# A bias row multiplied in the indexer's first visit, the last query heads turned one chunk later, one output part stored from ScalarE's queue

## The chip, the core and the metric

The kernel runs on one core of a Trainium2 chip. The core has five engines that run side by side, each through its own list of instructions in order: TensorE (PE, matmuls; its weight loads are shown apart as PEld), VectorE (DVE), ScalarE (ACT), GpSimd (POOL) and SyncE (SP, which here only issues DMAs). They meet in semaphores: an instruction can wait until a semaphore has reached a value, and can raise one when it ends. The metric is the device time of one execution in microseconds (us), lower is better.

## What is computed

Two transformer-like blocks in float32 over 256 rows of 2048 numbers. The first block has three branches (a windowed mean, a short convolution, and attention over the 64 keys that an indexer scores highest), gates, an output projection and an MLP. The second has attention with a Fourier mix beside it, and a last norm. What the change touches:

```
# block 1: the bias of a head depends on the distance of query and key alone
dist = q_pos[None, :, None] - idx
bias = table[t5_bucket(dist)]                      # table is rel_bias, 32 buckets x 8 heads
...
# block 1: the indexer
dots = einsum('bthd,bsd->bths', q_idx, k_idx)
score = einsum('bth,bths->bts', w_idx * IDX_HEADS ** -0.5, relu(dots))
...
# block 2
q = rope(rmsnorm(heads(p, OFF_Q, 12), q_norm_g), cos, sin) * q_scale
y = fft.fftn(u_b, axes=(rows, 128 columns of a group), norm="ortho").real
...
return rmsnorm(xs, final_g)                        # 256 x 2048, the output
```

## The kernel before

**Chunks.** All large products are cut into jobs of 512 weight columns, and a job into chunks of 256 weight rows (KC = 2 tiles of 128). `chunks` is the list of all of them, `q` is a chunk's number; `of[name].first` and `of[name].end` are the numbers of a job's first chunk and of the one behind its last. The weights of a chunk are loaded by SP into one of five buffers `raw`, in the order of the list `loads`, in which the 96 loads of `w_ada_2` (ada loads) stand between the others. ScalarE rounds them to float32r (`high`, tile `whiW` or `whiT`), VectorE subtracts that from them (`low`, tile `wloW` or `wloT`), and TensorE multiplies high by high, high by low and low by high: three matmuls for one product (lines 876 to 878, or 869 to 871 where the rows are the stationary side). One chunk of the first kind is 24 matmuls of 256 columns.

**The ring.** There are four pairs of high and low buffers. ScalarE's `high(q)` waits until the chunk four before it is multiplied (`s_pe`) and until its load has landed. SP's load of an entry waits until the entry five before it in `loads` has been read by VectorE (`s_lo` for weights, `s_ada` for an ada load). The loops of ScalarE and VectorE run three chunks ahead (AHEAD = 3): in step q each does first the side work that its table lists for q, then `high(q + 3)` or `low(q + 3)`, then what an ada load calls for (`ada`, four operations of 512 columns), then the end of a job. TensorE does the side work of q just ahead of chunk q.

**Side work.** Three tables written out by hand, `pe_at`, `act_at` and `dve_at`, say in which step a small piece stands. The pieces that the change touches or that stand beside them:

- `bias_row`: one float32 matmul of the 32 x 8 table with a 32 x 384 one-hot matrix (`oneh`, loaded by GpSimd at the start) gives the bias of every distance in bank 4. VectorE copies it to `erow` (line 1345) and raises `s_erow_v`, GpSimd stores it to HBM (line 556) and raises `s_erow_w`, and later GpSimd spreads it into a table (line 560) and loads that (line 564).
- `index_dots(u)`, `index_relu(u)`, `index_sum(u)`: the indexer in twelve units, two to a visit, from chunk `of["vw"].end + 1` = 33 on, every four chunks. Unit 0 of `index_dots` waits for `s_erow_v`, since it writes the bank that the bias row stood in; unit 0 of `index_sum` waits for `s_erow_w`, since the scores `sc` lie where `erow` lay.
- `turn_qk(s, tt)`: four 128 x 128 transposes that turn the heads of a query job; `s == 4` is the job `qq2`, the last four heads. They are first used by `scores2(8)`, in step `of["ga0"].first + 3`.
- `fourier_t(g)` and `fourier_d(g)`: the two products of the Fourier mix of a group.

"Visit" is used here for a stretch in which TensorE leaves the chunks for side work.

**The end.** The last chunks are `o23`. VectorE and ScalarE scale the rows of `X2` by the last norm's factor, `s_fin` counts VectorE's parts and `s_fina` ScalarE's (line 1220), and SP stores five parts (line 514), each as its wait is met, in the order in which they are listed.

Of the kernel before, what the change touches and what calls it, by code (L numbers as in the profile page):

```python
# [132 lines left out]
def program(nc, a, out, scratch_e, scratch_x):  # L133
    ctx = ExitStack()
    with ctx:
# [5 lines left out]
        chunks, of, given = [], {}, [0, 0]  # L141
# [29 lines left out]
        pe_at, act_at, dve_at = defaultdict(list), defaultdict(list), defaultdict(list)  # L171

        def side(table, q, part, *arg):
            table[q].append((part, arg))
# [7 lines left out]
        for u in range(3, 8):  # L182
            side(act_at, u - 2, "turn_x", u)
            side(dve_at, u - 2, "turn_x", u)
        side(pe_at, 7, "bias_row")
        side(dve_at, 8, "bias_row")
        units = [(1, par, i) for par in range(2) for i in range(4)] + [(0, par, i) for par in range(2) for i in range(2)]
        for u in range(12):
            q = of["vw"].end + 1 + 4 * (u // 2)
# [6 lines left out]
        for g in range(4):  # L196
            q = of["vw"].end + 11 + 4 * g
# [7 lines left out]
        for i in range(4):  # L205
            q = of["q1"].end + 2 + 10 * i
# [18 lines left out]
        for tt in range(2):  # L225
            q = of["wo0"].first + 3 + 2 * tt
# [3 lines left out]
            q = of["wo3"].end + 1 + tt  # L230
# [3 lines left out]
            q = of["dn33"].end + 1 + tt  # L234
            side(dve_at, q, "mlp_add", tt)
            q = of["dn33"].end + 2 + tt
# [8 lines left out]
        for s, name in enumerate(("kc", "k", "qq0", "qq1", "qq2")):  # L245
            q = of[name].end
            for tt in range(2):
                side(act_at, q + tt, "scale_qk", s, tt)
                if s:
                    side(dve_at, q + tt, "rotate", s, tt)  # L250
                side(pe_at, q + (7 if s == 3 else 5), "turn_qk", s, tt)
                side(act_at, q + (7 if s == 3 else 5), "turn_qk", s, tt)
        heads2 = [of["za0"].first + 6, of["qq1"].first + 5, of["za1"].end, of["zb"].first + 1, of["ga0"].first + 3, of["ga0"].first + 10]
        for i in range(6):
            q = heads2[i]
# [10 lines left out]
        for g in range(4):  # L266
            q = of["zb"].end + 2 + 3 * g
# [13 lines left out]
        def at(name, shape, off, dt=F32):  # L281
            return nc.alloc_sbuf_tensor_at(name, shape, dt, offset=off)
# [36 lines left out]
        a5 = tmp[5]  # L319
# [8 lines left out]
        def bg(name, shape, kb, dt=F32):  # L328
            return at(name, shape, big + int(kb * 1024), dt)
# [18 lines left out]
        x0 = bg("x0", [128, 2, 2048], 52)  # L348
        yah, yal = bg("yah", [128, 8, 256], 52, F32R), bg("yal", [128, 8, 256], 60, F32R)
        cm = bg("cm", [128, 2, 256], 68)  # L350
        oneh = bg("oneh", [128, 384], 70)
        vst = bg("vst", [128, 128], 71.5)
        quart = bg("quart", [128, 8, 2, 16], 70.5)
        foldm = bg("foldm", [128, 128], 71.5)
# [1 line left out]
        erow = bg("erow", [128, 384], 22)  # L356
# [40 lines left out]
        bank = [ctx.enter_context(nc.psum_tensor(f"ps{i}", [128, 512], F32)) for i in range(8)]  # L397
# [9 lines left out]
        def sem(name):  # L407
            return ctx.enter_context(nc.semaphore("s_" + name))
# [16 lines left out]
        s_turn, s_turned, s_oper = sem("x_turned"), sem("x_scaled"), sem("x_operand")  # L425
        s_skew, s_erow, s_erow_v, s_erow_w, s_bt = sem("bias_copies"), sem("bias_row"), sem("bias_row_read"), sem("bias_row_stored"), sem("bias_table")
# [23 lines left out]
        s_fgb, s_o2v, s_o2sq, s_o2g, s_fin, s_fina = (  # L450
            sem("final_gain"), sem("x3_rows"), sem("x3_square"), sem("x3_gained"), sem("out_rows0"), sem("out_rows1"))
        s_out = [sem(f"out{i}") for i in range(5)]
# [10 lines left out]
        def norm_col(name, tt):  # L463

            w = 4 if name in QK else 1
            c = col(f"n_{name}{tt}", 2 * w)
            return c[:, 0:w], c[:, w:2 * w]
# [5 lines left out]
        @block.sync  # L473
        def _(sp):
            def rows_of(x, tt):
                return a[x][0, 128 * tt:128 * tt + 128, :]

            for t in range(2):
                sp.dma_start(x0[:, t, :], rows_of("x", t)).then_inc(s_x[t], 16)
            sp.dma_start(ident[:, :], a["k_ident"]).then_inc(s_ident, 16)  # L480
            sp.dma_start(vst[0:64, :], a["norm_gains"].rearrange("l g (r c) -> (l g r) c", c=128)).then_inc(s_va, 16)
            sp.dma_start(vst[64:112, :], a["b_gate"].rearrange("l g (r c) -> (l g r) c", c=128)).then_inc(s_va, 16)
            for i, (kind, m) in enumerate(loads):
                if i == 4:
                    r0 = 0
                    for name, n, pat in (("pool_scale", 8, "l (r c) -> (l r) c"), ("conv_w", 24, "l k (r c) -> (l k r) c"),
                                         ("norm_g_2", 16, "l (r c) -> (l r) c"), ("q_norm_g_2", 1, None), ("k_norm_g_2", 1, None),
                                         ("c_2", 16, "l (r c) -> (l r) c"), ("c_ctx_2", 16, "(r c) -> r c")):
                        sp.dma_start(vsu[r0:r0 + n, :], a[name] if pat is None else a[name].rearrange(pat, c=128)).then_inc(s_vb, 16)
                        r0 += n  # L490
                    sp.dma_start(vsu[82:114, :], a["b_ada_2"][:, 0:4096].rearrange("l (r c) -> (l r) c", c=128)).then_inc(s_vb, 16)
                if i >= NRAW:
                    was, mm = loads[i - NRAW]
                    if was == "w":
                        sp.wait_ge(s_lo, mm + 1)
                    else:
                        sp.wait_ge(s_ada, mm + 1)
                if kind == "w":
                    job, k = chunks[m]
                    o = 0  # L500
                    for c0, cn in job.cols:
                        sp.dma_start(raw[i % NRAW][:, 0:KC, o:o + cn], job.w[:, k:k + KC, c0:c0 + cn]).then_inc(s_raw[i % NRAW], 16)
                        o += cn
                else:
                    j, k = m // 8, m % 8 * KC
                    wa = a["w_ada_2"][0].rearrange("(k p) n -> p k n", p=128)
                    sp.dma_start(raw[i % NRAW][:, :, :], wa[:, k:k + KC, 512 * j:512 * j + 512]).then_inc(s_raw[i % NRAW], 16)
            rows = out[0].rearrange("(t p) n -> p t n", p=128)
            for i, (tt, c0, c1) in enumerate(((0, 1536, 2048), (0, 0, 1536), (1, 1536, 2048), (1, 0, 768), (1, 768, 1536))):
                if i == 3:  # L510
                    sp.wait_ge(s_fina, 1)
                else:
                    sp.wait_ge(s_fin, (1, 2, 3, 0, 4)[i])
                sp.dma_start(rows[:, tt, c0:c1], X2[:, tt, c0:c1]).then_inc(s_out[i], 16)
            for i in range(5):
                sp.wait_ge(s_out[i], 16)
# [112 lines left out]
        def _(pe):  # L629
# [43 lines left out]
            def bias_row():  # L673
                pe.wait_ge(s_oneh, 16)
                pe.wait_ge(s_relb, 16)
                pe.wait_ge(s_oper, 8)
                pe.matmul(bank[4][0:8, 0:384], a5[0:32, 0:8], oneh[0:32, :], start=True, stop=True).then_inc(s_erow, 1)

            def ada_fold():

# [235 lines left out]
        def _(act):  # L916
# [287 lines left out]
            def ep_o2(job, b0, b1):  # L1204
                c = job.arg
                for tt in range(2):
                    if c == 3 and tt == 1:
                        for i in range(2):
                            act.wait_ge(s_o2v, 8 + i)
                            act.activation(tmp[3][:, 256 * i:256 * i + 256], X2[:, 1, 1536 + 256 * i:1792 + 256 * i], ACT.Square,  # L1210
                                           accum_out=col("x3_halves")[:, i:i + 1]).then_inc(s_o2sq, 1)
                        break
                    act.wait_ge(s_o2v, 2 * c + tt + 1)
                    act.activation(tmp[2 * (c % 2) + tt][:, :], X2[:, tt, 512 * c:512 * c + 512], ACT.Square,
                                   accum_out=ss_all[:, 2, tt, c:c + 1]).then_inc(s_o2sq, 1)
                if c == 3:
                    act.wait_ge(s_rstd, norm_no["x3", 1])
                    act.wait_ge(s_o2g, 6)
                    x = X2[:, 1, 0:768]
                    act.activation(x, x, ACT.Copy, scale=norm_col("x3", 1)[1]).then_inc(s_fina, 1)  # L1220

            eps = {"copy": ep_copy, "kk": ep_kk, "vw": ep_vw, "pool": ep_pool, "cu": ep_cu, "cb": ep_cb, "gate": ep_gate, "br": ep_br,
                   "wo": ep_wo, "up": ep_up, "dn": ep_dn, "qk": ep_qk, "v": ep_v, "silu": ep_silu, "gate2": ep_gate2, "pa": ep_pa, "o2": ep_o2}
# [6 lines left out]
            for i in range(3):  # L1230
# [4 lines left out]
                if i == 1:  # L1235
                    act.wait_ge(s_rstd, 2)
                    x = x0[:, 1, 512:1024]
# [14 lines left out]
        def _(v):  # L1252
# [89 lines left out]

            def bias_row():
                v.wait_ge(s_erow, 1)
                v.tensor_copy(erow[0:8, :], bank[4][0:8, 0:384]).then_inc(s_erow_v, 1)

            def index_sum(u):
                tt, par, i = units[u]
# [511 lines left out]
```

## Time and profile before

| what | value |
|---|---|
| median of three executions | 2211.5 us (2211.46 to 2211.52) |
| profiled execution, its own time | 2211.45 us |
| its span in the profile | 2209.7 us |
| TensorE busy | 2200.9 us, 100% of the span |
| VectorE busy | 1503.4 us, 68% |
| ScalarE busy | 1066.5 us, 48% |
| GpSimd busy | 63.1 us, 3% |
| share of TensorE in the chain that ended last | 99% |

How to read it: the profile shows one execution. A row of the timeline gives start, duration, engine, line of the kernel, what is written and read, how many instructions were put together, and in square brackets how long the engine sat idle just before and what ended that. Matmuls overlap in their pipeline, so the distance between two starts is what one costs, not its duration. The span is what the profile covers; 1.8 us of the execution lie outside it.

### The profile page before, as it was taken

Reading aid. Unit: us, or ns where it says so; the run is one execution under the profiler, and the core shown is the slowest. Engines: PE = TensorE matmul, PEld = TensorE weight load, DVE = VectorE, ACT = ScalarE, POOL = GpSimd, SP = SyncE. Lnnn points to the kernel's source line nnn. Section 1 sums busy time; section 2 is a strip of 40 time slices with the busy share of each in tenths; the row PEclk is TensorE's granted clock in tenths of the full one; section 3 lists DMA queues with packets and bytes.
Section 4 is the critical chain, followed back from the end, with each engine's and each line's share of the span. In section 5 each row is a group of like instructions: output and inputs, shape, how many; then the busy total and the mean of one; then the engine's idle time right before and its main releaser. Section 6 shows DMA issues by size and latency. Waiting matters only on the chain.

```text
span 2209.7 us, 37880 instructions
## 1 busy us (share of the span) xinstructions
PE 2200.9 (100%) x16074; PEld 2069.7 (94%) x16074; DVE 1503.4 (68%) x1901; ACT 1066.5 (48%) x1417; POOL 63.1 (3%) x72
## 2 busy tenths in 40 slices
PE   9999999999999999999999999999999999999998
PEld 9999999999999889989988988988889999999987
DVE  7789588888889657544554555555756556577776
ACT  5444445544444546444443443444656555544443
POOL 1000000000000000000000000000100000010001
PEclk9999999999999999999999999999999999999999
DMA  8876676787787756656656666666664445678784
GB/s 275 241 224 209 192 248 219 231 281 259 252 277 269 234 181 186 196 191 190 200 191 194 188 200 202 196 195 200 227 204 139 135 144 171 213 265 294 252 279 157
DMA packets 248034, 474.99 MB, mean 215 GB/s; under 512 B 21527, under 2 KB 26001, under 8 KB 247097
## 3 DMA queue, kind: packets, MB, share of 16 engines
q1 hardware_dynamic: 243032, 454.40, 64.4%
q0 software_dynamic: 4832, 18.16, 2.5%
q8 instruction: 126, 2.06, 0.4%
q14 instruction: 44, 0.35, 0.0%
HBM read 468.30 MB, written 5.78 MB: 215 GB/s over the span
## 4 chain that ended last, share of the span: by engine, by line
PE 99%; issue 0%; DVE 0%; ACT 0%; POOLq 0%; POOL 0%; DVEq 0%
PE ps L876 21%; PE ps L878 21%; PE ps L877 21%; PE ps L869 11%; PE ps L870 11%; PE ps L871 11%; PE ps L793 1%; PE ps L697 1%; PE ps L666 0%; PE ps L782 0%; PE ps L890 0%; PE ps L772 0%; PE ps L773 0%; PE ps L709 0%; PE ps L755 0%
## 5 line engine op out<-in xcount | busy, mean ns | idle before, releaser
L876 PE MATMUL ps<-op0h,whiW 128*128 128x256 f32 x3376 | 937.5, 278 | 0.0
L878 PE MATMUL ps<-op0h,wloW 128*128 128x256 f32 x3376 | 932.3, 276 | 0.0
L877 PE MATMUL ps<-op0l,whiW 128*128 128x256 f32 x3376 | 932.2, 276 | 0.0
L1263 DVE TENSOR_TENSOR wloW<-raw,whiW 128x1024 fp32r<-128x1024 f32 (+1 forms) x503 | 611.1, 1226 | 342.3 <-ACT whiW L923 339.9
L923 ACT ACTIVATE whiW<-raw 128x1024 fp32r<-128x1024 f32 (+1 forms) x504 | 529.4, 1058 | 582.1 <-PE ps L878 479.3
L876 PEld LDWEIGHTS ps<-op0h,whiW 128*128 128x128 f32 x3376 | 633.7, 188 | 2.2 <-issue 1.6
L877 PEld LDWEIGHTS ps<-op0l,whiW 128*128 128x128 f32 x3376 | 633.8, 188 | 0.6
L878 PEld LDWEIGHTS ps<-op0h,wloW 128*128 128x128 f32 x3376 | 633.7, 188 | 0.0
L1263 DVE TENSOR_TENSOR wloT<-raw,whiT 128x1024 fp32r<-128x1024 f32 (+1 forms) x264 | 317.4, 1212 | 258.8 <-ACT whiT L923 258.2
L923 ACT ACTIVATE whiT<-raw 128x1024 fp32r<-128x1024 f32 (+1 forms) x264 | 273.8, 1047 | 293.3 <-PE ps L871 244.1
L869 PE MATMUL ps<-whiT,op1h 128*128 128x512 f32 x640 | 249.2, 389 | 0.0
L870 PE MATMUL ps<-wloT,op1h 128*128 128x512 f32 x640 | 249.0, 389 | 0.0
L871 PE MATMUL ps<-whiT,op1l 128*128 128x512 f32 x640 | 249.0, 389 | 0.0
L1291 DVE SCALAR_TENSOR_TENSOR tmp<-raw,csil,tmp 128x512 f32<-128x512 f32 x300 | 209.4, 747 | 2.5 <-DMA raw<-in_w_ada 1.3
L871 PEld LDWEIGHTS ps<-whiT,op1l 128*128 128x128 f32 x640 | 120.1, 188 | 25.0
L869 PEld LDWEIGHTS ps<-whiT,op1h 128*128 128x128 f32 x640 | 120.1, 188 | 24.8
L870 PEld LDWEIGHTS ps<-wloT,op1h 128*128 128x128 f32 x640 | 120.1, 188 | 24.7
L876 PE MATMUL ps<-op1h,whiW 128*128 128x256 f32 x512 | 142.0, 277 | 0.0
L877 PE MATMUL ps<-op1l,whiW 128*128 128x256 f32 x512 | 141.4, 276 | 0.0
L878 PE MATMUL ps<-op1h,wloW 128*128 128x256 f32 x512 | 141.4, 276 | 0.0
L877 PEld LDWEIGHTS ps<-op1l,whiW 128*128 128x128 f32 x512 | 96.1, 188 | 0.1
L876 PEld LDWEIGHTS ps<-op1h,whiW 128*128 128x128 f32 x512 | 96.1, 188 | 0.1
(286 smaller groups left out, 2041.8 us busy)
## 6 DMA issues: line engine op xcount, KB each, us to landing
raw<-in_w_in SPq DMA_DIRECT2D x256, 512.0 KB, 4.4
raw<-in_w_up SPq DMA_DIRECT2D x128, 512.0 KB, 3.8
raw<-in_w_down SPq DMA_DIRECT2D x128, 512.0 KB, 3.8
raw<-in_w_ada SPq DMA_DIRECT2D x96, 512.0 KB, 4.6
raw<-in_w_gate SPq DMA_DIRECT2D x96, 512.0 KB, 5.1
raw<-in_w_out SPq DMA_DIRECT2D x64, 512.0 KB, 5.0
raw<-in_w_branch SPq DMA_DIRECT2D x48, 512.0 KB, 4.9
raw<-in_w_proj_a SPq DMA_DIRECT2D x24, 512.0 KB, 5.0
```

Of the source, the lines that this page charges most:

```text
L697: mm = pe.matmul(ps[:, j * nk:(j + 1) * nk], qb[lo:lo + 64, h // 2, 128 * tt:128 * tt + 128], kid[lo:lo + 64, 0:nk], start=True, stop=True)
L793: mm = pe.matmul(ps[:, 128 * tt:128 * tt + 128], vv[:, st % 2, 128 * kv:128 * kv + 128], p[:, 128 * st:128 * st + 128], start=st == 0, sto ...
L869: pe.matmul(o, th, h[:, kk, c0:c1], start=first, stop=False, skip_group_check=True)
L870: pe.matmul(o, th, l[:, kk, c0:c1], start=False, stop=False, skip_group_check=True)
L871: mm = pe.matmul(o, tl, h[:, kk, c0:c1], start=False, stop=last, skip_group_check=True)
L876: pe.matmul(o, wh, xh[:, ka, :], start=first and m % 2 == 0, stop=False, skip_group_check=True)
L877: pe.matmul(o, wh, xl[:, ka, :], start=False, stop=False, skip_group_check=True)
L878: mm = pe.matmul(o, wl, xh[:, ka, :], start=False, stop=last, skip_group_check=True)
L923: act.activation(whi[job.mode][q % NSPL][:, :, 0:job.n], raw[i][:, :, 0:job.n], ACT.Copy).then_inc(s_hi, 1)
L1263: v.tensor_tensor(wlo[job.mode][q % NSPL][:, :, 0:job.n], x, h.bitcast(F32), ALU.subtract).then_inc(s_lo, 1)
L1291: op = v.scalar_tensor_tensor(o, w, c, o, ALU.mult, ALU.add)
```

## The change

There are four edits. `bias_row` goes from step 7 to step 33 on TensorE (ahead of the first `index_dots`) and from step 8 to step 34 on VectorE, and writes bank 7 in place of bank 4; its wait for the x operand is dropped, and `oneh` gets another place in memory. `turn_qk` of the last heads goes from the fifth to the sixth chunk behind `qq2`, on TensorE and on ScalarE. The part of the output that ScalarE scales is stored by ScalarE itself. SP stores the other four.

```diff
-        side(pe_at, 7, "bias_row")
-        side(dve_at, 8, "bias_row")
+        side(pe_at, of["vw"].end + 1, "bias_row")
+        side(dve_at, of["vw"].end + 2, "bias_row")
...
-                side(pe_at, q + (7 if s == 3 else 5), "turn_qk", s, tt)
-                side(act_at, q + (7 if s == 3 else 5), "turn_qk", s, tt)
+                side(pe_at, q + (7 if s == 3 else 6 if s == 4 else 5), "turn_qk", s, tt)
+                side(act_at, q + (7 if s == 3 else 6 if s == 4 else 5), "turn_qk", s, tt)
...
-        oneh = bg("oneh", [128, 384], 70)
+        oneh = bg("oneh", [128, 384], 30.25)
...
-            for i, (tt, c0, c1) in enumerate(((0, 1536, 2048), (0, 0, 1536), (1, 1536, 2048), (1, 0, 768), (1, 768, 1536))):
-                if i == 3:
-                    sp.wait_ge(s_fina, 1)
-                else:
-                    sp.wait_ge(s_fin, (1, 2, 3, 0, 4)[i])
+            for i, (tt, c0, c1) in enumerate(((0, 1536, 2048), (0, 0, 1536), (1, 1536, 2048), (1, 768, 1536))):
+                sp.wait_ge(s_fin, i + 1)
...
                 pe.wait_ge(s_relb, 16)
-                pe.wait_ge(s_oper, 8)
-                pe.matmul(bank[4][0:8, 0:384], a5[0:32, 0:8], oneh[0:32, :], start=True, stop=True).then_inc(s_erow, 1)
+                pe.matmul(bank[7][0:8, 0:384], a5[0:32, 0:8], oneh[0:32, :], start=True, stop=True).then_inc(s_erow, 1)
...
                     act.activation(x, x, ACT.Copy, scale=norm_col("x3", 1)[1]).then_inc(s_fina, 1)
+                    act.wait_ge(s_fina, 1)
+                    act.dma_start(out[0, 128:256, 0:768], x).then_inc(s_out[4], 16)
...
                 v.wait_ge(s_erow, 1)
-                v.tensor_copy(erow[0:8, :], bank[4][0:8, 0:384]).then_inc(s_erow_v, 1)
+                v.tensor_copy(erow[0:8, :], bank[7][0:8, 0:384]).then_inc(s_erow_v, 1)
```

The line of `index_dots(0)` that waits for `s_erow_v` is not touched, nor that of `index_sum(0)` that waits for `s_erow_w`.

In the listings below a row gives line, operation, written tile, read tiles, size, and in brackets the semaphores it waits for. `s_bias_row` is `s_erow`, `s_bias_row_read` is `s_erow_v`, and `s_bias_row_stored` is `s_erow_w`.

TensorE at the step from chunk 32 to chunk 33, before (`kid,qb` is `index_dots`):

```order
670 L876 MATMUL ps<-op0h,whiW_55 128x256
671 L877 MATMUL ps<-op0l,whiW_55 128x256
672 L878 MATMUL ps<-op0h,wloW_63 128x256
673 L697 MATMUL ps<-kid,qb 128x256 [waits s_pair0_read,s_bias_row_read,s_pair1_read]
674 L697 MATMUL ps<-kid,qb 128x256 x3
675 L876 MATMUL ps<-op0h,whiW_57 128x256 [waits s_chunk_low]
```

The same place, after the change (the lines count four less):

```order
670 L873 MATMUL ps<-op0l,whiW_55 128x256
671 L874 MATMUL ps<-op0h,wloW_63 128x256
672 L673 MATMUL ps<-oneh,tmp_79 8x384 [waits s_rel_bias,s_oneh]
673 L693 MATMUL ps<-kid,qb 128x256 [waits s_pair0_read,s_bias_row_read,s_pair1_read]
674 L693 MATMUL ps<-kid,qb 128x256 x3
675 L872 MATMUL ps<-op0h,whiW_57 128x256 [waits s_chunk_low]
```

The bias matmul now stands directly ahead of the indexer's matmul that waits for its result to be read.

VectorE around the low part of chunk 36 (`wloW_63`), before; row 93 is the low part of chunk 35, rows 94 to 97 are an ada load's:

```order
91 L1588 TENSOR_SCALAR wi<-ps 128x16 [waits s_v1,s_chunk_done]
92 L1588 TENSOR_SCALAR wi<-ps 128x16 [waits s_v1]
93 L1263 TENSOR_TENSOR wloW_69<-raw_50,whiW_61 128x1024 [waits s_chunk_high]
94 L1291 SCALAR_TENSOR_TENSOR tmp_74<-raw_51,csil,tmp_74 128x512 [waits s_dve_step,s_raw2]
...
98 L1263 TENSOR_TENSOR wloW_63<-raw_52,whiW_55 128x1024 [waits s_chunk_high]
99 L1363 TENSOR_SCALAR sc<-tmp_76,wi 128x256 [waits s_index_relu,s_pair1_read,s_bias_row_stored]
100 L1365 SCALAR_TENSOR_TENSOR sc<-tmp_76,wi,sc 128x256 [waits s_dve_step]
101 L1263 TENSOR_TENSOR wloW_65<-raw_53,whiW_57 128x1024 [waits s_chunk_high]
```

The same place, after the change:

```order
92 L1261 TENSOR_TENSOR wloW_69<-raw_50,whiW_61 128x1024 [waits s_chunk_high]
93 L1289 SCALAR_TENSOR_TENSOR tmp_74<-raw_51,csil,tmp_74 128x512 [waits s_dve_step,s_raw2]
...
97 L1261 TENSOR_TENSOR wloW_63<-raw_52,whiW_55 128x1024 [waits s_chunk_high]
98 L1343 COPY erow<-ps 8x384 [waits s_bias_row]
99 L1361 TENSOR_SCALAR sc<-tmp_76,wi 128x256 [waits s_index_relu,s_pair1_read,s_bias_row_stored]
100 L1363 SCALAR_TENSOR_TENSOR sc<-tmp_76,wi,sc 128x256 [waits s_dve_step]
```

The copy of the bias row stands behind the low part of chunk 36, and directly ahead of the sum that waits for the stored row.

## Rows read from the trace of the kernel before

**Rows 1.** The page: TensorE's share of the span, and the chain that ended last.

```profile
PE 2200.9 (100%) x16074; PEld 2069.7 (94%) x16074; DVE 1503.4 (68%) x1901; ACT 1066.5 (48%) x1417; POOL 63.1 (3%) x72
PE 99%; issue 0%; DVE 0%; ACT 0%; POOLq 0%; POOL 0%; DVEq 0%
```

**Rows 2.** Timeline, TensorE: start, duration, engine, line, tiles; the bias row at chunk 7.

```profile
35.09 0.28 PE L878 MATMUL ps<-op0h,wloW 128*128 128x256 f32 x1
35.29 0.81 PE L677 MATMUL ps<-oneh,tmp 32*8 32x384 f32 x2
...
36.25 0.28 PE L877 MATMUL ps<-op0l,whiW 128*128 128x256 f32 x1
```

**Rows 3.** Timeline, TensorE: the indexer's first visit (chunk 33) and its third.

```profile
91.63 0.28 PE L878 MATMUL ps<-op0h,wloW 128*128 128x256 f32 x1
91.84 1.99 PE L697 MATMUL ps<-kid,qb 64*128 64x256 f32 x8
...
117.86 1.99 PE L697 MATMUL ps<-kid,qb 64*128 64x256 f32 x8
```

**Rows 4.** Timeline, VectorE: low part of chunk 32, an ada load, low part of 36.

```profile
85.86 1.23 DVE L1263 TENSOR_TENSOR wloW<-raw,whiW 128x1024 fp32r<-128x1024 f32 x1 [1.18 <-ACT whiW L923]
...
93.22 2.73 DVE L1291 SCALAR_TENSOR_TENSOR tmp<-raw,csil,tmp 128x512 f32<-128x512 f32 x4
96.39 1.23 DVE L1263 TENSOR_TENSOR wloW<-raw,whiW 128x1024 fp32r<-128x1024 f32 x1 [0.43 <-ACT whiW L923]
97.53 0.35 DVE L1363 TENSOR_SCALAR sc<-tmp,wi 128x256 f32<-128x256 f32 x1
```

**Rows 5.** Timeline, ScalarE: high parts of chunks 32 and 36.

```profile
84.77 1.06 ACT L923 ACTIVATE whiW<-raw 128x1024 fp32r<-128x1024 f32 x1 [0.84 <-PE ps L871]
...
95.29 1.06 ACT L923 ACTIVATE whiW<-raw 128x1024 fp32r<-128x1024 f32 x1 [4.26 <-DMA raw<-in_w_in]
```

**Rows 6.** The tile erow: VectorE's copy, GpSimd's store, and its time to landing.

```profile
L1345 DVE COPY erow<-ps x1: 535/535/535, 42.1 to 42.1; 8x384 f32<-8x384 f32 x1
L556 POOL DMA_DIRECT2D scratch_e<-erow x1: 538/538/538, 43.0 to 43.0; - x1
DMA to landing us min/median/max: 3.6/3.6/3.6
```

**Rows 7.** Stretches at the end: engines' busy time, granted clock (PEclk), DMA share, GB/s; below, the last matmul.

```profile
2202.00:2204.20 2.20, 0.21 (x2) 0.01 (x1) 1.72 (x6) 0.51 (x2) 0.13 (x1) 1.00 0.87 354
2204.20:2204.30 0.10, 0.00 (x0) 0.00 (x0) 0.00 (x0) 0.00 (x0) 0.10 (x1) 0.50 1.52 614
...
2201.93 0.28 PE L871 MATMUL ps<-whiT,mgl 128*128 128x256 f32 x1
```

**Rows 8.** Timeline, TensorE: the matmuls on zeros with which the program starts.

```profile
1.18 7.82 PE L890 MATMUL ps<-tmp 128*128 128x256 f32 x24 [1.18 <-DVE tmp L1805]
9.15 1.91 PE L890 MATMUL ps<-tmp 128*128 128x256 f32 x8
```

**Rows 9.** Timeline, TensorE: last matmul before, second after: a double visit, two single ones.

```profile
1818.11 0.28 PE L878 MATMUL ps<-op0h,wloW 128*128 128x256 f32 x1
...
1820.07 0.28 PE L877 MATMUL ps<-op0l,whiW 128*128 128x256 f32 x1
...
1825.32 0.28 PE L878 MATMUL ps<-op0h,wloW 128*128 128x256 f32 x1
...
1826.43 0.28 PE L877 MATMUL ps<-op0l,whiW 128*128 128x256 f32 x1
...
1828.94 0.28 PE L878 MATMUL ps<-op0h,wloW 128*128 128x256 f32 x1
...
1830.04 0.28 PE L877 MATMUL ps<-op0l,whiW 128*128 128x256 f32 x1
```

**Rows 10.** Timeline, the end: VectorE's last operation, and SP's last issue.

```profile
2205.06 0.61 DVE L1786 TENSOR_SCALAR X<-X,stat 128x768 f32<-128x768 f32 x1
2206.03 0.45 SPq L514 DMA_DIRECT2D out_dram<-X  x1
```

## The prediction

> **What bounds the kernel now.** I read the page first. TensorE is busy for the whole span and carries 99% of the chain that ended last; other engines' idle time costs nothing [rows 1]. So the questions are what the change adds to TensorE's list, where it makes TensorE wait, and what it does behind TensorE's last matmul. I then went along the timeline for the five places that the change touches: chunk 7, chunk 33, the two chunks behind `qq2`, and the end. TensorE's stream has no wait in it between the start and the end: matmuls of a chunk start 0.11 to 0.12 us apart throughout (24 in the 2.7 us of a chunk, worked out below from [rows 3]). A wait that is put in has therefore nothing later to be absorbed by, and counts in full.
>
> **The bias row at chunk 7.** From the last matmul before the visit to the second after it there are 36.25 - 35.09 = 1.16 us [rows 2]. Two regular distances of 0.115 are in this, so the visit costs 0.93 us. Its removal brings every later matmul of TensorE forward by 0.93 us, as far as the others follow.
>
> **The bias row at chunk 33.** Here the new order matters more than the matmul. Ahead of chunk 33 TensorE now multiplies the bias row and then at once reaches `index_dots(0)`, which waits for `s_erow_v`, VectorE's copy of that row. The copy stands in VectorE's list behind the low part of chunk 36. In the trace of before TensorE is at this visit at 91.84 [rows 3], while VectorE starts the low part of chunk 36 at 96.39 and the next instruction at 97.53 [rows 4]. VectorE is 5.7 us behind the point at which TensorE needs it. That has cost nothing so far, since TensorE had the low parts up to chunk 35 already.
>
> When does the copy end in the changed kernel? Going back from 97.53: the low part of 36 waits for the high part, and this waits 4.26 us for its load, landed at 95.29 [rows 5]. That load takes the buffer of the ada load that VectorE reads behind the low part of chunk 32 (85.86) [rows 4]. The low part of 32 follows ScalarE's high part at 84.77, which was released by TensorE [rows 5]. The whole chain thus hangs on TensorE's pace and should come 0.93 us earlier. Then the copy starts at 97.53 - 0.93 = 96.60. It takes 0.54 [rows 6], and I allow 0.1 for the semaphore to TensorE. `index_dots(0)` starts at 97.24 where it started at 91.84: **5.4 us later**. In that sum the gain at chunk 7 is used up, and the bias matmul itself (from 90.9 to some 91.7) lies within the wait. TensorE stands still for about 5.5 us.
>
> Bounds: if the load lands when it landed before, because the DMA engines and not TensorE's pace set it, nothing is won at chunk 7 for this chain, and the term is 6.3. If the load comes sooner than that, the ada load's four operations (93.22 plus 2.73 = 95.95, against a start of the low part at 96.39) still hold VectorE [rows 4], so at most 0.44 more is won: 5.0. I take 5.4, since both ends of the chain that I can see are released by TensorE.
>
> **Who else waits there.** Behind the copy VectorE reaches `index_sum(0)`, which waits for the stored row. GpSimd's issue began some 0.3 us after the copy ended, and the store landed 3.6 us after the issue [rows 6]: VectorE is held until 97.1 + 0.3 + 3.6 = 101.0, then comes a sum of 0.9 and the low part of chunk 37. But the high part of 37 waits for chunk 33 to be multiplied, and TensorE ends this chunk at 97.2 + 2.1 + 2.7 = 102.0. (A chunk takes (117.86 - 91.84 - 2 x 2.1) / 8 = 2.7 [rows 3]; 2.1 is a visit of 1.99 with its edges.) With 1.1 and 1.2 for high and low, the low part of 37 is there at about 104.5, and TensorE, which has four chunks in hand (33 to 36), needs it at 97.2 + 2.1 + 4 x 2.7 = 110.1. Price 0 while those four chunks cover it. Were the store to take 6 us longer, TensorE would begin to wait again.
>
> **The clock.** A standstill of TensorE can cost more than its length. At the end of the kernel the last matmul starts at 2201.93 and runs 0.28; the granted clock is 1.00 until 2204.2 and 0.50 behind it [rows 7]: it went from 2.4 to 1.2 GHz 2.0 us after TensorE had run out of work. The standstill at chunk 33 is nearly three times as long, so I expect the fall there as well. What it costs to come back is in the first matmuls: 24 records take 7.82 us from a cold start, where 8 of the same kind take 1.91 a little later [rows 8]. 7.82 - 3 x 1.91 = 2.1 us is what the slow stretch cost there. (The profile has no clock for that stretch of its own; the matmuls are slow by about two, as at 1.2 GHz.) Counted by starts (each row holds one last duration of 0.38 over the distances) it is 2.4. Bounds 0 (no fall) and 2.4; I take **2.1**, the nearest row being the same event.
>
> The Trainium skill (TensorE: Matmul & The Clock Gate, section on the HAM clock gate) says that the array falls to half its clock when it has idled and gets it back only after sustained work. By that rule the sum keeps the clock term; without it the time would be 2.1 us less. The trace agrees, with 2.0 us from the last matmul to 0.50 [rows 7].
>
> **The last heads' turns.** Do two pieces in one visit cost less than in two? The double visit of the Fourier mix takes 1820.07 - 1818.11 = 1.96, the visit with the turns 1.11, the one with `fourier_d(3)` alone 1.10 [rows 9]. Less two distances of 0.115 each, that is 1.73 against 0.88 + 0.87 = 1.75. A merged visit saves 0.02: nothing. The turns are used five chunks later in place of six, over 13 us, and ScalarE's two copies move by one chunk with its slack of three. 0.0, bounds -0.1 and +0.1.
>
> **The last store.** SP issues three stores in a row at the end, and the last issue starts at 2206.03, though its data were ready when VectorE ended at 2205.67 [rows 10]. With ScalarE issuing one, SP's last issue starts at about 2205.7, 0.35 earlier. ScalarE's copy ends at about the same time, and its issue should take SP's 0.45. No row shows ScalarE issuing a DMA; the nearest other queue is GpSimd's 0.54 [rows 6]. I take -0.3, bounds -0.4 and +0.3 (a slow first issue there, or transfers that share the DMA engines and land no sooner).
>
> The Trainium skill (DMA: Bandwidth & Descriptors, section on issuing engines) says that issuing from several engines saves only the sequencer's time to start a transfer. By that the term can't exceed the 0.45 of an issue.
>
> **The sum.** 5.4 + 2.1 + 0.0 - 0.3 = +7.2 us on the profiled execution's own 2211.45 (span 2209.7 and 1.8 around it), which is the median of the runs to 0.05. That gives **2218.6**.
>
> **Rivals.**
> 1. *The clock does not fall* at chunk 33. For it: the engine idles in the middle of dense work, not behind it. Against: 2.0 us were enough at the end. It gives 5.4 - 0.3 = +5.1, 2216.6. Chance 0.12: with the smaller standstill, 5.0, and the larger gain at the end it stays just above or at the bound of 4.4 us.
> 2. *Not slower: VectorE's copy is there in time.* The price of the wait is the distance between TensorE's arrival and the copy's end, and it would be zero if VectorE reached the copy by 91.7. It would have to be 5.4 us further in its list, that is, ahead of the ada load and the low part of 36 rather than behind them. Then only small terms are left: 0.93 less at chunk 7, at least 0.64 more (two records at 384 columns and their edges) at chunk 33, the store's -0.3. That gives -0.5, 2211.0. Against it speaks the order itself and a VectorE that is occupied there nearly without a pause. This mechanism decides only from a lead of five microseconds that no row shows. Chance 0.04, cases in which more than half of the wait vanishes included.
> 3. *A second wait*: VectorE, held by the store, is late with a low part between chunks 37 and 40, because the store lands late or VectorE can't make up for it. VectorE's margin is the 5.6 us worked out above. Should half of its 4 us hold come back at TensorE, the time is 2221. Chance 0.06.
>
> That the merged visits don't bring what a merger could bring is no rival but part of every case [rows 9].
>
> **Chances and range.** Forecast (standstill and fall of the clock) 0.78, giving 2217 to 2220.5 with its bounds; rivals 1, 2 and 3 have 0.12, 0.04 and 0.06. The range leaves out the cases without the wait and the far half of the second wait: 2216.1 to 2220.5. About 0.2% (4.4 us) is what a measurement can tell from no change. Slower by more than that: the forecast, the second wait, and three quarters of rival 1, 0.93. Within: the rest of rival 1 and most of rival 2, 0.06. Faster: 0.01, what is left of rival 2, since even without the wait the terms that I know do not reach 4.4.
>
> **What will show it.** TensorE idle ahead of line 693 for 5 to 6 us, released by VectorE's copy at line 1343; the copy directly behind the low part of chunk 36. A granted clock of 0.5 for a few microseconds from the middle of that idle time on, with matmul starts some 0.21 apart in place of 0.115. A double visit behind `qq2` of about 1.7 us. SP's last store issued some 0.35 us sooner relative to VectorE's last operation. The forecast is wrong if TensorE passes chunk 33 without a standstill, or if the time between chunk 33 and the end of TensorE's work changes by more than half a microsecond beyond the slow stretch.

## The result, and the profile after

| | before | after |
|---|---|---|
| median | 2211.51 us (2211.46 to 2211.52) | 2220.25 us (2219.36 to 2220.73) |
| ratio to before, 95% interval | | 1.0039 (1.0029 to 1.0050) |
| profiled execution, its own time | 2211.45 us | 2220.12 us |
| its span | 2209.7 us | 2218.3 us |

The medians are those of five executions each. The change makes the kernel 8.7 us slower, 0.4% of its time. The forecast was 2218.6 with a range of 2216.1 to 2220.5: the time lies in the range, 0.25 us below its upper end. The direction and the two mechanisms were as foreseen, the size of one of them was not. The five executions also scatter more than the five of before, over 1.4 us where it was 0.06. That contrast is overstated by so few executions: in the larger sets of the kernel before that the experiments are compared with (15 to 25 executions), the times lie over 0.4 to 0.9 us.

The page of the changed kernel, to be read against [rows 1]: busy time is nearly the same on every engine but TensorE, whose matmuls took 3 us more.

```profile
PE 2203.9 (99%) x16074; PEld 2072.4 (93%) x16074; DVE 1503.5 (68%) x1901; ACT 1067.0 (48%) x1417; POOL 63.2 (3%) x72
```

TensorE's waits in the changed kernel (engine, line, waited for, us in total, times, longest us). Before, only the second row was there; the third is in the start:

```profile
PE ps L693 <- DVE erow L1343: 5.0, 1, 5.0
PE ps L886 <- DVE tmp L1803: 1.2, 1, 1.2
PE ps L892 <- DMA vst<-in_b_gate: 0.6, 1, 0.6
```

The timeline of TensorE in the changed kernel at chunk 33, to be read against [rows 3]:

```profile
90.77 0.28 PE L874 MATMUL ps<-op0h,wloW 128*128 128x256 f32 x1
90.97 0.81 PE L673 MATMUL ps<-oneh,tmp 32*8 32x384 f32 x2
96.83 3.75 PE L693 MATMUL ps<-kid,qb 64*128 64x256 f32 x8 [5.05 <-DVE erow L1343]
100.51 0.58 PE L872 MATMUL ps<-op0h,whiW 128*128 128x256 f32 x1
100.89 0.41 PE L873 MATMUL ps<-op0l,whiW 128*128 128x256 f32 x1
...
113.26 0.28 PE L874 MATMUL ps<-op0h,wloW 128*128 128x256 f32 x1
113.47 1.99 PE L693 MATMUL ps<-kid,qb 64*128 64x256 f32 x8
...
2210.55 0.28 PE L867 MATMUL ps<-whiT,mgl 128*128 128x256 f32 x1
```

From the trace of before, the second matmul behind the first visit and the last matmul ahead of the next one:

```profile
93.98 0.28 PE L877 MATMUL ps<-op0l,whiW 128*128 128x256 f32 x1
...
104.65 0.28 PE L878 MATMUL ps<-op0h,wloW 128*128 128x256 f32 x1
```

Three things are in the changed kernel's rows. TensorE reaches the visit 0.86 us sooner (90.77 for 91.63), then stands still for 5.05 us until VectorE's copy, and starts the index matmuls at 96.83 where it was 91.84: 4.99 us later. And the same four float32 matmuls (two records each, so x8) take 3.75 us, where the next visit has 1.99.

VectorE there, to be read against [rows 4]: the copy (line 1343) stands behind the low part of chunk 36, and the next instruction is held by the stored row.

```profile
92.36 2.73 DVE L1289 SCALAR_TENSOR_TENSOR tmp<-raw,csil,tmp 128x512 f32<-128x512 f32 x4
95.01 1.22 DVE L1261 TENSOR_TENSOR wloW<-raw,whiW 128x1024 fp32r<-128x1024 f32 x1
96.14 0.54 DVE L1343 COPY erow<-ps 8x384 f32<-8x384 f32 x1
101.59 0.35 DVE L1361 TENSOR_SCALAR sc<-tmp,wi 128x256 f32<-128x256 f32 x1 [4.91 <-DMA scratch_e<-erow]
```

ScalarE's high part of chunk 36, which started at 95.29 before [rows 5]:

```profile
93.44 1.06 ACT L919 ACTIVATE whiW<-raw 128x1024 fp32r<-128x1024 f32 x1 [3.41 <-DMA raw<-in_w_in]
```

The clock of the changed kernel by stretches (stretch, its length in us, busy us and instructions of PE, PEld, DVE, ACT and POOL, then the granted clock as a share of 2.4 GHz, DMA share and GB/s):

```profile
91.80:94.00 2.20, 0.00 (x0) 0.00 (x0) 2.20 (x4) 0.56 (x1) 0.00 (x0) 1.00 0.95 329
94.00:94.20 0.20, 0.00 (x0) 0.00 (x0) 0.20 (x1) 0.20 (x1) 0.00 (x0) 0.98 1.16 379
94.20:96.80 2.60, 0.00 (x0) 0.00 (x1) 2.48 (x4) 0.30 (x1) 0.00 (x0) 0.50 0.97 328
96.80:104.40 7.60, 7.57 (x26) 6.39 (x27) 0.84 (x2) 1.20 (x2) 0.54 (x1) 0.50 0.41 143
104.60:106.00 1.40, 1.40 (x14) 1.40 (x13) 0.00 (x0) 0.55 (x1) 0.00 (x0) 1.00 0.00 0
```

The clock fell to 1.2 GHz 2.4 us after the bias matmul's end (91.78), and stayed there for 7.6 us and more of work, until about 104.5. How much it lost by that is read from the starts of its matmuls. Against before it is 4.99 us late at the index matmuls, 100.89 - 93.98 = 6.91 late at the second matmul behind them, and 113.26 - 104.65 = 8.61 late at the last matmul ahead of the next visit. So the slow clock cost 8.61 - 4.99 = **3.6 us**. From there to the end the delay stays what it is: the last matmul starts at 2210.55 for 2201.93 [rows 7], 8.62 late. The sum closes: 8.61 of the 8.67 us between the two profiled executions are there when chunk 36 is multiplied.

### The profile page after: what moved, and what is told of

Same layout as the page of the kernel before. It is cut to its first block, busy times and chain, and to the rows that moved or that the text cites. A ratio compares the mean times of both kernels' runs of the same rounds, so it can differ in the third digit from the quotient of the medians.

```text
span 2218.3 us, 37880 instructions
## 1 busy us (share of the span) xinstructions
PE 2203.9 (99%) x16074; PEld 2072.4 (93%) x16074; DVE 1503.5 (68%) x1901; ACT 1067.0 (48%) x1417; POOL 63.2 (3%) x72
## 4 chain that ended last, share of the span: by engine, by line
PE 99%; DVE 0%; DMA 0%; issue 0%; SPq 0%; ACT 0%; POOLq 0%; POOL 0%; DVEq 0%
PE ps L873 21%; PE ps L872 21%; PE ps L874 21%; PE ps L865 11%; PE ps L866 11%; PE ps L867 11%; PE ps L789 1%; PE ps L693 1%; PE ps L778 0%; PE ps L663 0%; PE ps L769 0%; PE ps L768 0%; PE ps L705 0%; DMA vst<-in_b_gate 0%; PE ps L751 0%
```

## The experiments

All runs are compared with runs of the kernel before on the same chip. Its medians there were 2211.47 to 2211.53.

**The bias row alone (bias_only).** The changed kernel with the turns and the stores put back as before.

```diff
-                side(pe_at, q + (7 if s == 3 else 6 if s == 4 else 5), "turn_qk", s, tt)
-                side(act_at, q + (7 if s == 3 else 6 if s == 4 else 5), "turn_qk", s, tt)
+                side(pe_at, q + (7 if s == 3 else 5), "turn_qk", s, tt)
+                side(act_at, q + (7 if s == 3 else 5), "turn_qk", s, tt)
...
-                    act.wait_ge(s_fina, 1)
-                    act.dma_start(out[0, 128:256, 0:768], x).then_inc(s_out[4], 16)
```

> Only the bias row is moved; turns and stores as before. If the standstill at chunk 33 and the slow clock behind it are the whole loss, this is 8.5 to 9.0 us over before, 2220.0 to 2220.5. If the turns or the store carry a part of it, it is less by that part.

Measured: 2220.22 us (2219.31 to 2220.62), ratio 1.0039 (1.0024 to 1.0054). The whole loss is in this one part. The timeline of TensorE and the clock in this kernel:

```profile
96.64 3.75 PE L696 MATMUL ps<-kid,qb 64*128 64x256 f32 x8 [5.05 <-DVE erow L1344]
```

```profile
94.60:104.80 10.20, 8.16 (x29) 6.98 (x30) 2.73 (x5) 1.20 (x2) 0.54 (x1) 0.50 0.51 170
```

The index matmuls are 96.64 - 91.84 = 4.80 us late. The last matmul starts at 2210.64, 8.71 late, so the slow clock costs 3.9 us here.

**The rest alone (rest_only).** The kernel before with the turns and ScalarE's store of the change.

> Only the turns and ScalarE's store are changed; the bias row as before. The trace of after has TensorE at the same 8.61 us of delay before and behind the merged visit, and the end no sooner, so this should stand within 0.1 us of before (2211.4 to 2211.6). The prediction's term for the store (-0.3) would give 2211.2; a cost hidden behind the standstill would show as 2211.8 or more.

Measured: 2211.57 us (2211.51 to 2211.80) against 2211.47, ratio 1.0000 (0.9991 to 1.0010). The interval of the ratio is some 2 us wide to either side and can't tell 0.3 us by itself, but none of the ten executions lies below 2211.51. The two other parts show no gain together; the -0.3 us of the prediction is not seen.

**The standstill filled (fill).** TensorE waits as long, but works while it does.

```diff
                 pe.matmul(bank[7][0:8, 0:384], a5[0:32, 0:8], oneh[0:32, :], start=True, stop=True).then_inc(s_erow, 1)
+                for i in range(11):
+                    pe.matmul(bank[6][:, 0:256], ident[:, :], op0h[:, 0, :].bitcast(F32), start=True, stop=True)
```

> The changed kernel with eleven float32 matmuls of 256 columns, whose result nothing reads, between the bias row and the first index_dots: about 11 x 0.43 = 4.7 us of work in a standstill of 5.05. If the slow clock is what costs 3.6 us beyond the wait, the clock stays at 1.00 and the time is before plus 5.0, 2216.3 to 2216.8. If VectorE and ScalarE are what is late after the wait, nothing changes and it stays at 2220.2.

Measured: 2216.43 us (2216.40 to 2217.09), ratio 1.0022 (1.0013 to 1.0032). This is before plus 4.96. The timeline of TensorE in this kernel, and below it the clock of the two stretches (each of the eleven float32 matmuls has two records, so the row says x22):

```profile
91.59 5.02 PE L675 MATMUL ps<-op0h,ident 128*128 128x256 f32 x22
97.39 1.96 PE L695 MATMUL ps<-kid,qb 64*128 64x256 f32 x8 [0.78 <-DVE erow L1345]
```

```profile
91.60:97.40 5.80, 5.02 (x24) 4.13 (x23) 5.05 (x7) 1.06 (x1) 0.00 (x0) 1.00 0.96 324
97.40:105.00 7.60, 7.60 (x58) 7.09 (x59) 2.06 (x3) 2.26 (x3) 0.54 (x1) 1.00 0.33 114
```

The index matmuls start even later than in the changed kernel (97.39, 5.55 us behind before), but take 1.96 us, and the delay at the last matmul is still 5.55. (This profiled execution, at 2217.09, is the longest of its kernel, so it is 5.55 there and 4.96 in the median.) VectorE is held by the stored row here too, for 3.86 us. So the 3.6 us beyond the wait are the clock's, and no other engine is late behind the standstill. The scatter is smaller too: six of the ten executions lie within 0.05 us of each other, and all ten within 0.7, as those of before do. That points to the clock as what made the changed kernel's executions differ.

**A shorter standstill (copy33).** VectorE's copy one step earlier, ahead of the low part of chunk 36.

```diff
-        side(dve_at, of["vw"].end + 2, "bias_row")
+        side(dve_at, of["vw"].end + 1, "bias_row")
```

> The changed kernel with VectorE's copy one step earlier, ahead of the low part of chunk 36: TensorE is released about 1.2 us sooner and stands still for 3.9 us in place of 5.05. Wait plus clock: if the clock falls all the same, 5.0 - 1.2 + 3.6 = +7.4, 2218.9; if the slow stretch gets shorter with the standstill, less, down to +3.8 (2215.3) without a fall.

Measured: 2219.37 us (2218.61 to 2219.51), ratio 1.0035 (1.0022 to 1.0047). The timeline of TensorE and the clock in this kernel:

```profile
95.64 3.75 PE L693 MATMUL ps<-kid,qb 64*128 64x256 f32 x8 [3.91 <-DVE erow L1343]
```

```profile
93.40:95.60 2.20, 0.00 (x0) 0.00 (x0) 2.20 (x5) 1.06 (x1) 0.00 (x0) 0.50 0.96 292
95.60:103.60 8.00, 7.96 (x28) 6.78 (x29) 1.86 (x3) 1.19 (x2) 0.54 (x1) 0.50 0.58 203
103.80:106.00 2.20, 2.20 (x21) 2.20 (x20) 0.46 (x1) 1.06 (x1) 0.00 (x0) 1.00 0.00 0
```

The standstill is 3.91 us, and the clock falls and stays at 0.5 for 8.0 us of work. The index matmuls are 95.64 - 91.84 = 3.80 late, the last matmul 2209.56 - 2201.93 = 7.63 late: the clock takes 3.8 of it. A standstill that is shorter by 1.1 us saves nothing of the clock's price in the trace. The median is 0.9 us below the changed kernel's, and 0.5 above the 2218.9 that was expected if the clock fell all the same.

**Half filled (fill5).** As fill, with five matmuls in place of eleven.

> The changed kernel with five of the eleven idle matmuls: 2.1 us of work, then some 2.9 us of standstill. The wait is the same +5.0. If any standstill of over 2 us costs the clock as at the end of the kernel, the time stays at 2219 to 2220.5; if the fall needs more than this, 2216.4 as with eleven.

Measured: 2218.55 us (2217.87 to 2219.70), ratio 1.0033 (1.0021 to 1.0045). The timeline of TensorE and the clock in this kernel:

```profile
91.61 2.43 PE L675 MATMUL ps<-op0h,ident 128*128 128x256 f32 x10
96.72 1.96 PE L695 MATMUL ps<-kid,qb 64*128 64x256 f32 x8 [2.69 <-DVE erow L1345]
```

```profile
94.20:96.70 2.50, 0.00 (x0) 0.01 (x1) 2.38 (x4) 0.30 (x1) 0.00 (x0) 1.00 1.00 366
96.70:98.80 2.10, 2.08 (x9) 1.59 (x10) 0.00 (x0) 0.68 (x2) 0.54 (x1) 1.00 0.96 328
99.00:102.20 3.20, 3.20 (x17) 3.20 (x17) 0.59 (x2) 0.32 (x1) 0.00 (x0) 0.50 0.37 141
102.40:105.00 2.60, 2.60 (x25) 2.60 (x25) 0.64 (x2) 1.06 (x1) 0.00 (x0) 1.00 0.00 0
```

Neither of the two outcomes that I had set down came out: the median lies between them, though two of the six executions are in the first (2219.61 and 2219.70). A standstill of 2.69 us costs the clock too, but the fall comes late, when TensorE has been at work again for 2.2 us, and is over after some 3.4. In this execution (2218.03) the clock cost 1.6 us (4.88 us late at the index matmuls, 6.48 at the end). The executions lie over 1.8 us, more than for the full standstill.

**Without the wait (nowait).** The wait for the copy is needed for bank 7, whose next user is `pool_weight(0)`, and no longer for banks 4 and 5.

```diff
                     pe.wait_ge(s_pair[of["kk"].pair], of["kk"].after)
-                    pe.wait_ge(s_erow_v, 1)
...
                 if g == 0:
                     pe.wait_ge(s_pw, 16)
+                    pe.wait_ge(s_erow_v, 1)
```

> The changed kernel, but the wait for VectorE's copy of the bias row stands ahead of the first pool_weight (which uses bank 7) and no longer ahead of index_dots(0) (banks 4 and 5). No standstill at chunk 33 and no fall of the clock: TensorE should be 0.1 to 0.3 us ahead of before, 2211.2 to 2211.5. If VectorE's hold by the stored row (4.9 us) then makes a low part between chunks 37 and 40 late, TensorE waits there for 1 to 3 us: 2212.5 to 2214.5.

Measured: 2211.37 us (2211.27 to 2211.86) against 2211.47, ratio 1.0000 (0.9990 to 1.0009). The timeline of TensorE in this kernel at chunk 33, and of VectorE:

```profile
90.84 0.81 PE L673 MATMUL ps<-oneh,tmp 32*8 32x384 f32 x2
91.58 1.99 PE L692 MATMUL ps<-kid,qb 64*128 64x256 f32 x8
...
93.72 0.28 PE L873 MATMUL ps<-op0l,whiW 128*128 128x256 f32 x1
```

```profile
96.01 0.54 DVE L1343 COPY erow<-ps 8x384 f32<-8x384 f32 x1
101.01 0.35 DVE L1361 TENSOR_SCALAR sc<-tmp,wi 128x256 f32<-128x256 f32 x1 [4.46 <-DMA scratch_e<-erow]
```

The place of one line is the whole difference between 2220.25 and 2211.37. TensorE is 0.26 us ahead behind the visit (93.72 for 93.98), and keeps that to the end. VectorE is still held for 4.46 us, and TensorE does not wait for it in this trace: the hold, which the third rival is about, was covered by the chunks in hand.

**Without the hold as well (free).** As nowait, with `erow` in memory of its own, so that `index_sum(0)` needs no wait for the stored row.

```diff
-        erow = bg("erow", [128, 384], 22)
+        erow = bg("erow", [128, 384], 20.375)
...
                 if u == 0:
-                    v.wait_ge(s_erow_w, 16)
```

> The changed kernel with neither wait: the one for the copy stands ahead of pool_weight as in nowait, and erow lies where nothing else does, so that index_sum(0) no longer waits for the stored row. VectorE isn't held for the 4.5 us. If that hold never reached TensorE, the time is that of nowait, 2211.3 to 2211.4.

Measured: 2211.38 us (2211.30 to 2211.66) against 2211.52, ratio 1.0000 (0.9991 to 1.0009). The same as nowait: by the medians, VectorE's hold did not reach the end.

**The turns alone (turn_only)** and **the store alone (store_only)**, each as the change has it, in the kernel before.

> Only the turns of the last heads one chunk later. The double visit costs 1.96 to 2.0 us where the two cost 2.2 less one edge: no difference by the trace, 2211.4 to 2211.5. If the turns carry the 0.1 us by which turns and store together stood over before, 2211.57.

> Only ScalarE's own store of its part is changed. SP's last issue starts 0.33 us sooner relative to the end of TensorE's work in the trace of after, but the two last transfers took 3.3 and 3.6 us to land in place of 3.0. By that, no gain: within 0.1 us of before, 2211.4 to 2211.6. The prediction's -0.3 would give 2211.2. If another queue costs something outside the span, 2211.6 or more.

Measured: the turns 2211.50 us (2211.39 to 2211.89) against 2211.53; the store 2211.65 us (2211.58 to 2212.44) against 2211.52. Both ratios have 1 in their interval (0.9991 to 1.0009 and 0.9992 to 1.0010). The merged visit in the trace of the changed kernel:

```profile
1836.66 0.28 PE L874 MATMUL ps<-op0h,wloW 128*128 128x256 f32 x1
1836.78 1.04 PE L751 MATMUL ps<-ident,rot 128*128 128x128 f32 x8
1837.65 1.03 PE L811 MATMUL ps<-tmp,cdt 128*128 128x256 f32 x4
1838.33 0.47 PE L872 MATMUL ps<-op0h,whiW 128*128 128x256 f32 x1
1838.63 0.28 PE L873 MATMUL ps<-op0l,whiW 128*128 128x256 f32 x1
```

It takes 1838.63 - 1836.66 = 1.97 us, or 1.74 without two regular distances, where the two single ones took 1.75 [rows 9]. And the stores of the changed kernel, from its timeline and from the page's list of DMA issues (KB each, us to landing):

```profile
2213.79 0.86 SPq L511 DMA_DIRECT2D out_dram<-X  x2
2214.24 0.41 ACTq L1218 DMA_DIRECT2D out_dram<-X  x1
```

```profile
out_dram<-X ACTq DMA_DIRECT2D x1, 384.0 KB, 3.6
out_dram<-X SPq DMA_DIRECT2D x1, 384.0 KB, 3.3
```

SP's last issue starts at 2214.32 where 2206.03 + 8.62 = 2214.65 would be the old place, 0.33 us sooner, as predicted [rows 10]. But the two transfers of 384 KB took 3.6 and 3.3 us to land where they took 2.8 and 3.1, and the gain is used up. The last one landed at 2206.03 + 3.1 = 2209.1 before; SP's and ScalarE's of the changed kernel, put back by 8.62, landed at 2209.0 and 2209.2. The medians put the store at 0.1 us of loss; with the intervals given this is a tendency and not shown.

**The bias row in an earlier visit (early6).** The kernel before with the row in the visit of step 6, behind its transposes, in bank 2; chunk 8 waits for the copy. The wait for the x operand is dropped here as in the change.

```diff
-        side(pe_at, 7, "bias_row")
-        side(dve_at, 8, "bias_row")
+        side(pe_at, 6, "bias_row")
+        side(dve_at, 6, "bias_row")
...
                     pe.wait_ge(s_vbt, 1)
+                    pe.wait_ge(s_erow_v, 1)
```

> The kernel before with the bias row in step 6 of TensorE, behind the transposes of that visit, in bank 2, and VectorE's copy in its step 6, with chunk 8 waiting for it. No visit of its own: if a merged visit saves its edges, 0.1 to 0.3 us less than before, 2211.2 to 2211.4. If the copy (about 36.0) or the matmul's place costs a wait, 2211.5 or more.

Measured: 2211.40 us (2211.29 to 2211.62) against 2211.53. TensorE is 0.05 us ahead in the trace at chunk 33, and 0.02 of that is there before the row's new place. No gain from the merger is shown.

**The row moved, the wait where it belongs, nothing else (row_alone).** This is nowait without the turns and the store.

> Only the bias row is moved, with the wait for its copy ahead of pool_weight as in nowait; turns and stores as in before. In the trace of nowait TensorE was 0.26 us ahead of before from chunk 33 on, and ScalarE's store alone stood 0.13 over before. So 0.2 to 0.3 us under before, 2211.2 to 2211.3, and under nowait.

Measured: 2211.28 us (2211.16 to 2211.88) against 2211.51, ratio 0.9999 (0.9990 to 1.0008). It is the lowest median of all, 0.2 us or 0.01% under before, and far below what the intervals can tell from no change. In its profiled execution, the longest of its eleven, TensorE once waited for VectorE, at the first `pool_weight`:

```profile
PE ps L708 <- DVE tmp L1413: 0.6, 1, 0.6
```

Behind it stands ScalarE, which waited for a load before that:

```profile
128.91 1.06 ACT L922 ACTIVATE whiW<-raw 128x1024 fp32r<-128x1024 f32 x1 [8.08 <-DMA raw<-in_w_in]
```

The high part at this place began at 122.89 in before and at 122.56 in free, where VectorE is not held, but at 126.16 in nowait, where it is. Between 90 and 134 us, SP's longest wait for VectorE to have read a buffer was 6.7 us here and 6.5 in nowait, 3.0 in before and in free. So VectorE's hold behind the stored row makes loads late some 25 us on, and in a single execution that reached TensorE.

## Why the prediction was right, and where it was off

**That TensorE would stand still at chunk 33: right.** The place, the releaser and the neighbours are as named. The copy was forecast for 96.60, it began at 96.14; `index_dots(0)` for 97.24, it began at 96.83. The term is 4.99 us where 5.4 was taken and 5.0 was the lower bound. The difference is the load of chunk 36. The prediction had it come 0.93 us sooner, with TensorE's pace; ScalarE's high part began at 93.44 for 95.29, 1.85 us sooner. So VectorE went from the ada load's operations (92.36 + 2.73 = 95.09) to the low part at 95.01, without the 0.43 us of waiting seen before. The bound of 5.0 was drawn for exactly this case, and the choice within the bounds was off by 0.4.

**The removal at chunk 7: right.** TensorE reached chunk 33 0.86 us sooner, 0.93 was forecast. The first chunk began 0.13 us later in this execution, so the removal itself brought 0.99.

**The clock: the mechanism right, the size wrong.** The step that failed is "what it costs to come back is in the first matmuls", with 2.1 us taken and 2.4 as the bound. It cost 3.6 us in the changed kernel, 3.9 in bias_only (8.71 late at the last matmul, 4.80 at the index matmuls) and 3.8 in copy33. The start of the program was taken for the same event, but the slow work behind a standstill was longer: 7.6 us in the changed kernel, 8.2 in bias_only, 8.0 in copy33, against some 4.8 (twice the loss of 2.4) at the start. Nor is the start one price: its 24 records, 7.82 us in before, took 7.15 in copy33 and 8.46 in row_alone. A price read from one event was taken for a bound, which it is not. This is why the time lies 1.65 us above the forecast: +1.5 from the clock, +0.35 from the store, -0.4 from the wait, 0.13 because the median lies above the profiled execution, and the rest is rounding. That the time is in the range all the same owes something to luck: the clock's term is 1.2 us above its bound, and the wait came out at its lower one, 1.3 below its upper.

**The turns: right**, 0.0. **The store: wrong.** -0.3 was taken and no gain is seen. The issue is sooner by what was forecast, but the term took the landing time of a transfer as fixed, and only its bound allowed for more. The page of the Trainium skill that was weighed there (DMA: Bandwidth & Descriptors, section "Issuing engines are not separate DMA queues") has DMAs of all issuing engines run on the same 16 DMA engines. The trace is in line with it, with 3.6 and 3.3 us to landing for 2.8 and 3.1.

**The rivals.** The first (the clock does not fall) is what fill makes true by force, and its 2216.6 is near what that kernel measured, 2216.43. The second (the copy is there in time) put 2211.0 on the kernel without the wait; nowait measured 2211.37. The third (a second wait behind VectorE's hold) did not happen in the changed kernel, whose list of TensorE's waits has one wait behind the start. Free, which takes the hold away, is no faster than nowait. The mechanism is real all the same: row_alone shows it once, with 0.6 us.

## What to carry to other kernels

When a step is moved next to its consumer, look up in the order of the third engine, the one that hands the result over, how far it is behind at that moment: here VectorE's copy stood five microseconds late in its own list, and a move that brought some 0.2 us in the trace of nowait turned into a loss of 8.7. When the step also gets another buffer, ask whom the old wait still protects; here it had lost its reason at that place, and moving one line gives the whole loss back. And in a kernel whose TensorE never rests, price a standstill with the clock that goes with it: here standstills of 3.91 and 5.05 us cost 3.6 to 3.9 us on top of their length and one of 2.69 us cost 1.6, while one of 0.78 us cost nothing more.

## What the runs showed of the hardware

In the three traces with a standstill of 3.9 to 5.05 us, the granted clock was 0.50 for the same time, 10.2 us: from 94.2 to 104.4 in the changed kernel, from 94.6 to 104.8 in bias_only, from 93.4 to 103.6 in copy33. What differed is how soon it fell: 2.4, 3.0 and 1.7 us after the bias matmul's end. TensorE had begun again inside the slow time, and the rest of it was slow work: 7.6, 8.2 and 8.0 us. The cost, 3.6, 3.9 and 3.8 us, is close to half of that. So the shorter standstill of copy33 saved nothing of the clock's price, because the clock also fell sooner there. This is a reading of three traces, and no run was made for it.

The fall can also come after the work has resumed: in fill5, behind 2.69 us of rest, it came 2.2 us into the work (98.9), and the clock was back 3.4 us later, at a cost of 1.6 us. Only one trace shows this. The price differs between executions of one kernel: those of the changed kernel lie over 1.4 us, those of fill5 over 1.8. What decides between 3.4 and 10.2 us stays open; no run here was made for it.
